# High and low parts of the head tokens as one stationary operand, and the keys of a head turned together, in a hybrid decoder step on one NeuronCore

## The reference, cut to what matters

```
z = rmsnorm(x) @ w_in                       # [u | q | f | i | gate], 512 columns each
y_pool = pooled windows of u (2, 4, 8, 16), times w_pool, times scale
y_rec  = gated linear attention over 4 heads of 128, then rmsnorm, times silu(gate)
x = x + [y_pool | y_rec] @ w_out            # "out projection", 1024 x 1024
a, b = rmsnorm(x) @ w_a, rmsnorm(x) @ w_b   # "up", 1024 x 2816 each
x = x + (gelu(causal_conv3(a)) * b) @ w_down   # "down projection", 2816 x 1024
y = rmsnorm(x)                              # and the new states
```

## Time and profile before

| | us |
|---|---|
| median of 3 runs | 2554.62 |
| lowest, highest | 2551.93, 2557.63 |
| the profiled execution | 2552.1 |
| its span, first to last instruction | 2550.3 |
| PE busy in the span | 2478.0 (97%) |
| mean granted clock of PE | 0.993 of full speed |

### The profile page before, as it was taken

The page is one execution under the profiler, slowest core; times in us unless marked ns, Lnnn a source line. Parts: engine busy times, 40 slices in busy tenths (PEclk is TensorE's granted clock), DMA queues, the critical chain, the costliest instruction groups (busy, mean ns, idle before and its releaser), DMA issues.

```text
span 2550.3 us, 36515 instructions
## 1 busy us (share of the span) xinstructions
PE 2478.0 (97%) x13263; PEld 2100.9 (82%) x13263; DVE 1187.0 (47%) x2307; ACT 726.6 (28%) x1467; POOL 407.7 (16%) x311
## 2 busy tenths in 40 slices
PE   7988999999999999999999999999999999999997
PEld 7878799998778888888887888888887887888886
DVE  6777474333348754222245874222246684222234
ACT  4324132222224332111233332111233342211133
POOL 2235255555540300000000110000000020000000
PEclk9989999999999999999999999999999999999999
DMA  7732467676767224555656424555656523555653
GB/s 246 255 117 75 148 235 262 249 252 244 274 247 263 103 103 178 184 195 184 236 194 238 164 83 154 197 192 186 234 198 214 201 99 132 189 190 188 231 202 133
DMA packets 145350, 489.03 MB, mean 192 GB/s; under 512 B 8881, under 2 KB 79778, under 8 KB 96025
## 3 DMA queue, kind: packets, MB, share of 16 engines
q1 hardware_dynamic: 136747, 482.58, 52.8%
q10 hardware_dynamic: 8472, 4.75, 0.6%
HBM read 375.45 MB, written 112.02 MB: 191 GB/s over the span
## 4 chain that ended last, share of the span: by engine, by line
PE 91%; DVE 3%; issue 2%; DMA 2%; ACT 1%; POOL 1%; SPq 0%; DVEq 0%; ACTq 0%
PE ps L580 23%; PE ps L582 23%; PE ps L581 23%; PE ps L646 12%; PE ps L817 3%; PE ps L627 1%; PE ps L842 1%; DMA w_both<-w_split 1%; PE ps L849 1%; PE ps L611 1%; POOL w_both L556 0%; DVE arena L2115 0%; PE ps L814 0%; PE ps L906 0%; DMA w_raw<-in_w_in 0%
## 5 line engine op out<-in xcount | busy, mean ns | idle before, releaser
L580 PE MATMUL ps<-h_hi,w_both 128*128 128x512 f32 (+1 forms) x1536 | 586.6, 382 | 2.7 <-issue 2.7
L582 PE MATMUL ps<-h_lo,w_both 128*128 128x512 f32 (+1 forms) x1536 | 583.1, 380 | 0.0
L581 PE MATMUL ps<-h_hi,w_both 128*128 128x512 f32 (+1 forms) x1536 | 579.5, 377 | 0.0
L582 PEld LDWEIGHTS ps<-h_lo,w_both 128*128 128x128 f32 x1536 | 288.7, 188 | 59.7
L581 PEld LDWEIGHTS ps<-h_hi,w_both 128*128 128x128 f32 x1536 | 288.6, 188 | 58.8
L580 PEld LDWEIGHTS ps<-h_hi,w_both 128*128 128x128 f32 x1536 | 288.3, 188 | 58.3 <-issue 3.6
L580 PE MATMUL ps<-w_both,act_hi 128*128 128x512 f32 (+1 forms) x748 | 297.4, 398 | 1.8 <-DVE x_tok L2197 1.8
L582 PE MATMUL ps<-w_both,act_hi 128*128 128x512 f32 (+1 forms) x748 | 296.1, 396 | 0.0
L581 PE MATMUL ps<-w_both,act_lo 128*128 128x512 f32 (+1 forms) x748 | 295.5, 395 | 0.0
L2274 DVE TENSOR_TENSOR act_lo<-arena,act_hi 128x512 fp32r<-128x512 f32 (+1 forms) x176 | 137.5, 783 | 329.9 <-ACT act_hi L1573 329.4
L646 PE MATMUL ps<-h_hi,w_both 128*128 128x304 f32 (+1 forms) x1664 | 285.3, 294 | 2.7 <-ACT arena L1379 1.7
(11 more groups left out here) (254 smaller groups left out, 3323.3 us busy)
## 6 DMA issues: line engine op xcount, KB each, us to landing
w_both<-w_split SPq DMA_DIRECT2D x288, 1024.0 KB, 4.8
w_split<-w_both SPq DMA_DIRECT2D x96, 1024.0 KB, 6.3
w_raw<-in_w_down SPq DMA_DIRECT2D x24, 512.0 KB, 4.3
w_raw<-in_w_a SPq DMA_DIRECT2D x22, 512.0 KB, 4.3
w_raw<-in_w_b SPq DMA_DIRECT2D x22, 512.0 KB, 4.3
w_raw<-in_w_in SPq DMA_DIRECT2D x20, 512.0 KB, 5.5
x_tok<-in_x_prompt SPq DMA_DIRECT2D x16, 512.0 KB, 6.9
arena<-in_x_prompt SPq DMA_DIRECT2D x16, 512.0 KB, 6.8
```

What stands on the lines that cost most here:

```text
L580: nc.tensor.matmul(out, lhs[0], rhs[0], start=first, stop=False)
L581: nc.tensor.matmul(out, lhs[1], rhs[0], start=False, stop=False)
L582: return nc.tensor.matmul(out, lhs[0], rhs[1], start=False, stop=last)
```

## The change

1. In block 0's out and down projections the head tokens' low part (48 columns, and 16 columns that aren't used) and high part (48 columns) lie side by side as one stationary operand of 112 columns, in `h_side` and `act_wide`. Two matmuls, by the high and by the low weights, take the place of three; the low-times-low term comes in as well. The result has the low part's rows on PSUM partitions 0 to 47 and the high part's on 64 to 111, and DVE adds both to the residual, in two instructions of 48x512 where there was one (`head_part`).
2. To fill the new operand, ACT's and DVE's writes are cut anew: in `pool_high` and `pool_low` (block 0) three instructions where there were two, in `down_low` two for each contraction tile (64 and 512 columns) where there was one (560).
3. In all four blocks the keys of a head are turned together: four transposes into the four quarters of bank 5 after the last step of the head before it, two copies of 256 columns on ACT where there were four of 128, and L849 waits for ACT only at the first tile of a head. L849 now writes columns 0 to 127 of bank 5.

```diff
+            def head_product(bank, both, w, first, last):
+                nc.tensor.matmul(ps[0:SIDE + HEAD, bank, :], both, w[0], start=first, stop=False)
+                return nc.tensor.matmul(ps[0:SIDE + HEAD, bank, :], both, w[1], start=False, stop=last)
+            def head_rows_product(bank, k, kk, w):
+                return head_product(bank, h_side[:, k, 0:SIDE + HEAD], [v[:, kk, :] for v in w], k == 0, k == KD - 1)
...
-                        last = token_product(ps[0:HEAD, bank(0, TILES), :], slice(0, HEAD), 2 * i + kk, kk, wslot(i, 2))
+                        last = head_rows_product(bank(0, TILES), 2 * i + kk, kk, wslot(i, 2))
...
-                def kd_transposed(i):
...
-                    nc.tensor.transpose(ps[:, 5, 0:P], kd[:, h % 2, win(w)], ident).then_inc(kdt_done, 1)
+                def kd_transposed(h):
+                    pe.wait_ge(kd_ready, 4 * b + h + 1)
+                    pe.wait_ge(qe_ready, 4 * b + h + 1)
+                    if not (isinstance(b, int) and h == 0):
+                        pe.wait_ge(s_ready, 16 * b + 4 * h)
+                    for w in range(TILES):
+                        last = nc.tensor.transpose(ps[:, 5, win(w)], kd_at(h, hd)[:, win(w)], ident)
+                    last.then_inc(kdt_done, 1)
...
-                    pe.wait_ge(kdt_ready, n + (2 if i + 1 < HEADS * TILES else 1))
-                    nc.tensor.matmul(ps[:, 5, P:2 * P], kd_tok[:, i % 2, :], v_tok[:, w, hc], start=True,
+                    if w == 0:
+                        pe.wait_ge(kdt_ready, 2 * (4 * b + h + 1))
+                    nc.tensor.matmul(ps[:, 5, 0:P], kd_token(w, hd), v_tok[:, w, hc], start=True,
                                      stop=True).then_inc(su_done, 1)
...
-                    if i + 1 < HEADS * TILES:
-                        kd_transposed(i + 1)
                     outputs(i)
...
+                    if i % TILES == TILES - 1 and i + 1 < HEADS * TILES:
+                        kd_transposed((i + 1) // TILES)
...
+                            if t == TILES:
+                                last = head_product(down_bank(n, t, hd), act_wide[:, kk, 0:SIDE + HEAD], ws, first, fin)
+                                continue
...
-                        nc.scalar.activation(h_hi[:, g, FRONT], ps[:, 6, 0:CUT], ACT.Copy, scale=sc)
+                        nc.scalar.activation(h_side[:, g, SIDE:2 * SIDE], ps[:, 6, 0:SIDE], ACT.Copy, scale=sc)
+                        nc.scalar.activation(h_hi[:, g, HEAD:CUT], ps[:, 6, HEAD:CUT], ACT.Copy, scale=sc)
...
-                    nc.scalar.copy(kd_tok[:, i % 2, :], ps[:, 5, 0:P]).then_inc(kdt_ready, 1)
+                def kd_tokens(h):
+                    act.wait_ge(kdt_done, 4 * b + h + 1)
+                    if not (isinstance(b, int) and h == 0):
+                        act.wait_ge(su_done, 16 * b + 4 * h)
+                    for half in range(2):
+                        nc.scalar.copy((kd_late[1 - hd] if half else kd_tok)[:, :, :],
+                                       ps[:, 5, 2 * half * P:2 * (half + 1) * P].rearrange("p (a b) -> p a b", a=2)
+                                       ).then_inc(kdt_ready, 1)
...
-                    if i + 1 < HEADS * TILES:
-                        kd_tokens(i + 1)
+                    if w == 0:
+                        kd_tokens(h)
...
+            def head_part(c, bank, side, ready=None):
+                x = x_tok[0:HEAD, TILES, c]
+                last = v.tensor_tensor(x, x, ps[side:side + HEAD, bank, :], ALU.add)
+                if side:
+                    own.mark(last)
+                else:
+                    last.then_inc(ready, 1)
...
+                if hd:
+                    head_part(c, to(TILES), SIDE)
                 for t in range(TILES):
                     v.tensor_tensor(x_tok[:, t, c], x_tok[:, t, c], ps[:, to(t), :], ALU.add).then_inc(ready, 1)
                     if hd and t == 0:
-                        v.tensor_tensor(x_tok[0:HEAD, TILES, c], x_tok[0:HEAD, TILES, c],
-                                        ps[0:HEAD, to(TILES), :], ALU.add).then_inc(hready, 1)
+                        own.settle()
+                        head_part(c, to(TILES), 0, hready)
...
-                    v.tensor_tensor(act_lo[:, kk, lo:WIDE],
-                                    acts[:, bass.ds(2 * i + kk, 1), lo:WIDE].rearrange("p a b -> p (a b)"),
-                                    act_hi[:, kk, lo:WIDE].bitcast(F32), ALU.subtract).then_inc(act_lo_ready, 1)
+                    for out, cols in ((act_wide, slice(0, SIDE)), (act_lo, slice(HEAD, WIDE)))[1 - hd:]:
+                        last = v.tensor_tensor(out[:, kk, cols],
+                                               acts[:, bass.ds(2 * i + kk, 1), cols].rearrange("p a b -> p (a b)"),
+                                               act_hi[:, kk, cols].bitcast(F32), ALU.subtract)
+                    last.then_inc(act_lo_ready, 1)
```

More of the change, by code:

```diff
@@ L183, in trunk_step @@
         g_end = sb("g_end", [P, HEADS, TILES])
+        with nc.sbuf_tensor("h_side", [P, KD, 2 * SIDE], F32R) as h_side:
+            pass
         arena = sb("arena", [P, 24956])
@@ L238, in trunk_step @@
         kd = part(21854, 2, BLOCK)
+        kd_late = (part(22366, 2, P), x_tok[:, TILES, 5 * P:7 * P].rearrange("p (a b) -> p a b", a=2))
         qe = part(22878, 2, BLOCK)
@@ L670, in token_tiles @@
                             out = ps[:, banks[t], :] if t < TILES else ps[0:HEAD, hbank, :]
-                            last = token_product(out, cols, 2 * i + kk, kk, w)
+                            if t == TILES and u0 == U_OUT:
+                                last = head_rows_product(hbank, 2 * i + kk, kk, w)
+                            else:
+                                last = token_product(out, cols, 2 * i + kk, kk, w)
                     last.then_inc(unit_done, 1)
@@ L742, in second_out_unit @@
                                 y_turned(0, 1, turned)
-                        out, cols = (ps[:, banks[t], :], main(t)) if t < TILES else (
-                            ps[0:HEAD, banks[t], :], slice(0, HEAD))
-                        last = token_product(out, cols, 2 + kk, kk, wslot(1, 2))
+                        if t < TILES:
+                            token_product(ps[:, banks[t], :], main(t), 2 + kk, kk, wslot(1, 2))
+                        else:
+                            last = head_rows_product(banks[t], 2 + kk, kk, wslot(1, 2))
                 last.then_inc(unit_done, 1)
@@ L1128, in ktile @@
                                 pe.wait_ge(x2_ready, 8 * b + 2)
[L1129 to L1132 removed]
+                            ws = [w[:, slot, wk * 512:(wk + 1) * 512] for w in (w_hi, w_lo)]
+                            if t == TILES:
+                                last = head_product(down_bank(n, t, hd), act_wide[:, kk, 0:SIDE + HEAD], ws, first, fin)
+                                continue
+                            last = three(ps[:, down_bank(n, t, hd), :], (act_hi[:, kk, main(t)], act_lo[:, kk, main(t)]),
+                                         ws, first, fin)
                         return last
```

60 lines of the change are left out of this document (30 added, 30 removed).

## The result

The changed kernel takes 2537.9 us (median of 6 runs) against 2553.3 for the kernel before on the same chip: a ratio of 0.9933, 95% interval 0.9921 to 0.9945. One of the six took 2721.2 us at a granted clock of 0.845; the ratio leaves it out, and the median of the other five is 2536.0. The prediction was 2534.5, in a range of 2526 to 2543. The profiled executions have spans of 2534.3 and 2550.3 us, so 16.0 went where the sum had 20.1. The document goes through the stages, since most of the difference lies in two of them.

A forecast was written before the change was run, and what follows sets the result against it. PE, busy 97% of the span, was taken as the bound. Gains of 8.2 + 3.6 + 3.8 + 4.5 = 20.1 us off the profiled 2552.1 gave 2532.0, plus 2.5 for the median 2534.5; range 2526 to 2543.

The forecast's parts named there:

- Matmuls that go: Block 0: one head matmul in three goes, 0.233 us each, 10.25 in the down projection and 3.73 in the out projection.
- rival 5: Weights' arrival, not head matmuls, sets the down projection's pace; 2543.4 us, chance 0.06.
- Out projection: Block 0's out projection: 3.73 us of head matmuls less 0.1 for the added addition, 3.6 gained.
- Blocks 1 to 3: Attention of these blocks: fewer waits for ACT, less new waits at heads' starts; 1.5 us a block, 4.5 in all.
- Down projection: Block 0: 10.25 us of matmuls, less 0.65 longer wait between halves, less 1.4 for the split low part: 8.2.
- Block 0's attention: Moving the keys gives 3.8 us: 2.4 before step 4's masks, about 0.7 at each of two later gate tiles.
- These 2.4 come back: Block 0's attention: PE's stops of 1.49 and 0.9 us ahead of a gate tile, before step 4's masks, are regained.
- The clock: Whole kernel: as many low-clock stretches after PE's stops as before, at 1.6 us each, so nothing in the sum.
- Rival 2: One more low-clock stretch at the bundled waits, 1.6 us, 2536.1; three more, 2539.3; chance 0.10.
- rival 1: The attention stages of all blocks give nothing back; 11.8 us off, 2542.8; chance 0.13.
- rival 3: The attention gives nearly all and added instructions cost nothing; 32.4 us off, 2522.2; chance 0.05.
- Rival 4: Down projection: split low parts collide with POOL, PE stands 2.8 us per such tile; 2578 at 16 tiles; chance 0.04.

The follow-up runs named there:

- runs 3 to 9: Seven follow-up kernels, each the changed kernel with further edits, its out projection left as it was; ratios 0.9912 to 0.9955 of the kernel before.
- run 2: Kernel before with only the head tokens' high and low parts in one operand, the keys turned as before; 0.9971 of the kernel before.
- run 1: Kernel before with only the keys of a head turned together, the head tokens' products as before; 0.9970 of the kernel before.
- run 3: Changed kernel with token tiles 0 and 1 added ahead of the head rows between halves of block 0's down projection; 0.9944 of the kernel before.
- run 6: run 3 plus DVE's low parts of contraction tiles 2 and 3 ahead of the small norm instructions in block 0; 0.9926 of the kernel before.
- run 7: Changed kernel with the 64 head columns' low part behind the main tokens', on a semaphore only head matmuls wait for; 0.9926 of the kernel before.
- run 8: Changed kernel with the edits of run 6 and run 7, and block 0's second gate tile behind step 5; 2534.6 us, 0.9918 of the kernel before.

## Why the prediction held, and where its sum did not

- **Matmuls that go**: right. 60 pairs in place of 60 threes, at the spacing of the earlier trace rows; no wait for weights in the down projection, so rival 5 fell. The price was a little high: a contraction tile without a stop takes 3.26 us where it took 3.47, and the 38 tiles beside the places named under the down projection are 8.3 us shorter in all, 0.22 each. That makes 9.6 for 44 tiles, not 10.25.
- **Out projection**: 3.6 predicted; the out stage gave 3.1 and the stretch behind it 1.0, in which the stop of 1.87 is 1.39 now. That is 4.1 in this profile, but 2.3 to 4.9 in runs 3 to 9 and 1.1 in run 2. So "the full 3.73 less 0.1 gets through" isn't shown: where PE waits for POOL's weights, and how long, differs from profile to profile. That 4.1 is so near to 3.6 is partly luck.
- **Blocks 1 to 3**: 4.5 predicted, 1.6 + 1.8 + 1.7 = 5.1 measured, and run 1 has 4.6 from the keys alone. The stop for the state stays at 1.77 as said; the stop at a head's start is 0.24 (854.40 to 854.86 less 0.22) where 0.38 was worked out. No low stretch fell into these blocks in this profile; in run 3 and runs 6 and 7 one did, and cost a block its gain.
- **Down projection**: 8.2 predicted, 5.7 measured. Besides the 9.6, three terms were mis-sized. "PE's wait grows by 0.65" became 1.20: the added head rows, and in front of them the added low-part instruction, 1.05 long behind POOL. "I take 1.4 in all" for the split low part: the two stops of 0.20 and 1.06 with their tails cost 1.7. And the clock, 0 in the sum: two stretches in place of one, 14 matmuls 0.2 apart more in place of 8, 1.1. 9.6 - 1.2 - 1.7 - 1.1 = 5.6.
- **Block 0's attention**: 3.8 predicted, 0.9 measured from DVE's row on and 1.2 to the stage's end. "These 2.4 come back": 2.0 did, since the masks of step 4 began 8.04 us behind DVE's row (191.11 less 183.07) where it was 10.06 (193.39 less 183.33), each time with one low stretch ahead. Of "0.7 at each of the two later gate tiles", 0.8 came up to the sum of step 9 where the clock stayed up (DVE's wait there was 3.53 before, 2.95 in run 6), and 0.4 at the third. "ACT's and DVE's third instruction for each pooled group is in that figure": it is not covered and costs 0.7 at the stage's end. These make 2.5, as worked out under the table, and one low stretch more took 1.6 of it. The forecast of waits at heads' starts, "none in block 0", was wrong: there is one wait of 1.48, of head 1.
- **The clock** is the step that failed: "as many stretches as before". There was one more in the attention and one more between the halves, 1.6 and 1.1 of the 5.1 us by which the two stages fell short. Rival 2 had the price, 1.6, about right. Whether its chance of 0.10 was too low, these runs can't say: with the same stops the count differs from profile to profile, and each kernel has only one. So it is not shown that the longer stops brought the added stretches; that such a stretch costs 1.6 us is. The time still lies in the range because the out projection and blocks 1 to 3 gave 1.1 more, in part by luck, and because the range reached to rivals 1 and 5. Of the other cases, rival 1 (nothing from the attention) and rival 3 (nearly all) both fell, since the attention stages gave 0.9 and 5.1.
- **Rival 4**, the collisions: its mechanism was seen, and often, 12 of 44 instructions of 64 columns at 1 us or more and one at 2.40. What didn't come is PE's stop behind them, but for two: in the other tiles the lengthened pair stayed within the cover that the other buffer's matmuls give. The Trainium skill's page SBUF — State Buffer (SBUF: two separate sides) calls the port pair of VectorE and GpSimd a lock held for a whole instruction; the row at 708.86 agrees, since it ends with POOL's.

## What to carry to other kernels

When an edit gathers several short waits of PE into one long one, price the clock behind it as a risk: here a stretch cost 1.6 us, as much as the waits that were saved in a block, and it came behind the same stop in some profiles and not in others. An added instruction on an engine off the path costs what stands behind it in that engine's order, so ask what PE waits for behind it, and put that first; and when one link of such a chain is shortened, look for the next link (run 3) before counting the gain. Compare two profiles stage by stage between matmuls, since a stage that no edit touches differed by 4.6 us from one execution to another.

## What the runs showed of the hardware

- The same stop of 2.74 us was followed by a low clock in the changed kernel and in runs 3 and 7, and by the full clock in runs 1 and 6; stops of 2.40, 2.26 and 1.54 between the halves by the full clock (runs 3, 8, 6), and one of 1.77 before by the lower. In blocks 1 to 3 the same stop of 1.77 was followed by the full clock in the changed kernel and by the lower one in block 1 of run 3.
- POOL's subtraction in the weight split (L569) lengthened DVE's instructions on SBUF alone (64 columns: 0.23 to 2.40 us; 5 columns: 0.17 to 2.24), while additions that read PSUM kept their time: in run 6 two of 48 rows took 1.40 together and two of 128 rows 1.27 beside POOL's instruction of 2.40 us from 675.33 on.
